# Up projection in groups of 512 columns over two sets of four PSUM banks

## The reference

```python
def conv_ffn(h, w_up, conv_w, conv_b, w_down):     # h (256, 2048), w_up (2048, 11264), w_down (5632, 2048)
    S = h.shape[1]
    u = h @ w_up
    up = jnp.pad(u, ((0, 0), (CONV_WIDTH - 1, 0), (0, 0)))          # CONV_WIDTH = 3
    u = sum(conv_w[j] * up[:, j:j + S] for j in range(CONV_WIDTH)) + conv_b
    a, b = jnp.split(u, 2, axis=-1)
    return (jax.nn.silu(a) * b) @ w_down
...
h = rms_norm(x, ffn_norm[l])
x = x + conv_ffn(h, w_ffn_up[l], ffn_conv_w[l], ffn_conv_b[l], w_ffn_down[l])
```

## Time and profile before

| | |
|---|---|
| median of 3 runs | 1080.18 us |
| profiled execution | 1080.29 us, span 1078.6 us |
| TensorE matmul busy | 1073.7 us (100%) |
| VectorE busy | 908.6 us (84%) |
| ScalarE busy | 633.9 us (59%) |
| DMA | 260.77 MB, mean 242 GB/s |
| up projection | 367 to 857 us of the span |
| down projection | 857 to 1075 us of the span |

### The profile page before, as it was taken

The page is one execution under the profiler, slowest core; times in us unless marked ns, Lnnn a source line. Parts: engine busy times, 40 slices in busy tenths (PEclk is TensorE's granted clock), DMA queues, the critical chain, the costliest instruction groups (busy, mean ns, idle before and its releaser), DMA issues.

```text
span 1078.6 us, 18188 instructions
## 1 busy us (share of the span) xinstructions
PE 1073.7 (100%) x6543; PEld 928.9 (86%) x6543; DVE 908.6 (84%) x1376; ACT 633.9 (59%) x930; POOL 79.8 (7%) x114
## 2 busy tenths in 40 slices
PE   9999999999999999999999999999999999999998
PEld 9888888888888889888888988888888888888887
DVE  7878988889655678888888888888877889999997
ACT  7677676757554655545555555545555566656663
POOL 4500000000000000000000000000000000000000
PEclk9999999999999999999999999999999999999999
DMA  8656687777889888798888888889888789798884
GB/s 275 183 163 176 190 229 223 216 223 222 234 258 245 278 236 235 240 256 239 249 232 243 237 255 245 227 258 247 271 240 235 218 282 319 256 309 315 260 289 163
DMA packets 192336, 260.77 MB, mean 242 GB/s; under 512 B 9605, under 2 KB 143894, under 8 KB 192022
## 3 DMA queue, kind: packets, MB, share of 16 engines
q1 hardware_dynamic: 176246, 216.24, 62.4%
q0 software_dynamic: 13344, 38.80, 17.6%
q10 hardware_dynamic: 2688, 5.00, 1.2%
HBM read 255.02 MB, written 43.78 MB: 277 GB/s over the span
## 4 chain that ended last, share of the span: by engine, by line
PE 99%; DMA 1%; DVE 0%; SPq 0%; issue 0%; DVEq 0%
PE bank L1821 38%; PE bank L1829 20%; PE bank L2216 7%; PE bank L2215 7%; PE bank L2214 7%; PE bank L2067 3%; PE bank L1868 3%; PE bank L2068 3%; PE bank L2069 3%; PE bank L1869 3%; PE bank L1870 3%; PE bank L1789 1%; PE bank L1897 1%; DMA xt<-in_x_dram 1%; PE bank L2106 0%; PE bank L1986 0%
## 5 line engine op out<-in xcount | busy, mean ns | idle before, releaser
L792 ACT CAST w_hi<-raw 128x1024 fp32r<-128x1024 f32 x299 | 311.9, 1048 | 252.7 <-PE bank L1829 118.4
L1201 DVE TENSOR_TENSOR w_lo<-raw,w_hi 128x1024 fp32r<-128x1024 f32 x299 | 363.8, 1222 | 108.1 <-ACT w_hi L792 107.5
L1821 PE MATMUL bank<-hs,w_hi 128*128 128x512 f32 x1792 | 423.0, 391 | 0.0
L1821 PEld LDWEIGHTS bank<-hs,w_hi 128*128 128x128 f32 x1792 | 331.3, 188 | 66.2 <-issue 0.9
L1829 PEld LDWEIGHTS bank<-hs,w_lo 128*128 128x128 f32 x1792 | 224.6, 192 | 5.7 <-issue 0.2
L1829 PE MATMUL bank<-hs,w_lo 128*128 128x256 f32 x1792 | 227.3, 283 | 0.0
L1171 ACT CAST hi_slot<-slot 128x1024 fp32r<-128x1024 f32 (+1 forms) x102 | 117.7, 1187 | 64.7 <-DVE slot L1746 25.2
L1728 DVE TENSOR_TENSOR slot_lo<-slot,hi_slot 128x1024 fp32r<-128x1024 f32 (+1 forms) x102 | 136.7, 1388 | 5.8 <-ACT hi_slot L1171 4.7
L2216 PE MATMUL bank<-hi_slot,gated 128*128 128x512 f32 (+1 forms) x194 | 75.1, 387 | 0.0
L2214 PE MATMUL bank<-hi_slot,gated 128*128 128x512 f32 (+1 forms) x194 | 75.1, 387 | 0.0
L1646 DVE SCALAR_TENSOR_TENSOR C<-U,cols,C 128x256 f32<-128x256 f32 x176 | 73.3, 478 | 0.0
(11 more groups left out here) (248 smaller groups left out, 1183.8 us busy)
## 6 DMA issues: line engine op xcount, KB each, us to landing
raw<-in_w_ffn_up_dram SPq DMA_DIRECT2D x176, 512.0 KB, 5.2
u_sums<-in_w_ffn_down_dram POOLq DMA_DIRECT2D x58, 512.0 KB, 6.7
raw<-in_w_in_dram SPq DMA_DIRECT2D x51, 512.0 KB, 4.5
slot<-in_w_ffn_down_dram SPq DMA_DIRECT2D x38, 512.0 KB, 5.0
slot<-u_sums SPq DMA_DIRECT2D x74, 256.0 KB, 5.6
raw<-in_w_in_dram SPq DMA_DIRECT2D x66, 256.0 KB, 4.2
raw<-in_w_out_dram SPq DMA_DIRECT2D x32, 512.0 KB, 5.7
u_sums<-u_sums POOLq DMA_DIRECT2D x16, 512.0 KB, 7.4
```

The lines of the kernel that those rows point to most:

```text
L792: act.copy(w_hi[:, i, :], raw[:, i, :]).then_inc(units_hi, 1)
L1201: dve.tensor_tensor(w_lo[:, i, :], raw[:, i, :], w_hi[:, i, :].bitcast(F32), ALU.subtract)\
L1821: m = pe.matmul(banks[b][:, :], w_hi[:, i, c], hs[:, 4 * i + k, :], start=(first and k == 0), stop=(final and k == 3))
```

## The change

The up projection is done in 11 pairs of groups. Four quads make a pair: two for a (512 channels), two for b. A wide quad is half of the 2048 rows by 512 columns (a unit is 2 row tiles by 512 columns, loaded in rows of 2 KB), so that the two quads of a add up in four banks (2, 3, 6, 7), and those of b in the other four (0, 1, 4, 5). The number of units, of matmuls and their sizes stay as they are. The last pair's b is done as before: two quads of 256 columns and all rows (groups 20 and 21), each into two banks. The works follow in the order a, a, b, b of a pair; the work with number w holds the splitting of quad w+3 (before: w+2), and the first three quads are split ahead of work 0. `C` has three tiles instead of two. Since a result is whole only after two quads, works w and w+1 of a both wait for the end of the second quad. The loops of ScalarE and VectorE are written out. TensorE's loop has 9 passes of four quads. In the down projection pair 0 adds up in banks 2, 3, 6, 7 and pair 1 in 0, 1, 4, 5; TensorE now waits ahead of q = 0 for the evacuations of a, and ahead of q = 0 to 3 for the `gated_lo` that they need. Ahead of the loop TensorE waits for the row of the second norm (`row_made`), which is now spread through bank 0.

```diff
-        C = sb_at(place, "C", [P, 2, 2, SEQ])
+        C = sb_at(place, "C", [P, 3, 2, SEQ])
+        banks_up = [[(bank[2], bank[3]), (bank[6], bank[7])], [(bank[0], bank[1]), (bank[4], bank[5])]]
+        banks_row = [bank[6], bank[0]]
-        sums_of = [[bank[4], bank[5], bank[6], bank[7]], [bank[0], bank[1], bank[2], bank[3]]]
+        sums_of = [[bank[2], bank[3], bank[6], bank[7]], [bank[0], bank[1], bank[4], bank[5]]]
...  # SyncE
-            with sp.Fori(0, UP_GROUPS) as g:
-                load_channels(g * 2 + Q_UP, w_up_v, g * GC)
-                load_channels(g * 2 + Q_UP + 1, w_up_v, g * GC + D_FF)
+            def load_wide(n, ab):
+                for half in range(2):
+                    for i in range(RING):
+                        load_unit(n * 4 + Q_UP + 2 * ab + half, i, w_up_v, 8 * half + 2 * i, 2, n * GT + ab * D_FF, GT)
+            with sp.Fori(0, UP_PAIRS - 1) as n:
+                for ab in range(2):
+                    load_wide(n, ab)
+            load_wide(UP_PAIRS - 1, 0)
+            for half in range(2):
+                load_channels(Q_DOWN - 2 + half, w_up_v, D_FF + (UP_GROUPS - 2 + half) * GC)
...  # ScalarE
+            for n in range(UP_PAIRS):
+                for g in (2 * n, 2 * n + 1):
+                    a_work(g, 2 * n + g)
+                    if g - 1 in range(RESIDENT_SUMS, SEVENS) and g % 2 == 0:
+                        park_sums(g - 1)
+                for g in (2 * n, 2 * n + 1):
+                    if g == UP_GROUPS - 1:
+                        act.wait_ge(sum_parked, 16 * PARKED_SUMS)
+                    b_work(g, 2 * n + g + 2)
...
+            def some_hi(quad, units):
+                for i in units:
+                    if quad < Q_DOWN + 2:
+                        make_hi(quad, i)
...  # VectorE
+            def taps(work, c_tile, ab, g, quad):
                 dst = U[:, :, 2:SEQ + 2]
+                last_narrow = ab == 1 and g == UP_GROUPS - 2
+                evacuate(banks_up[ab][g % 2], work, (Q_UP + 2 * (work // 2) + 2 - last_narrow) * RING, dst)
+                some_lo(quad, [0])
...
+            def b_work(g, work):
+                quad = work + Q_UP + 3
+                taps(work, 1, 1, g, quad)
                 dve.wait_ge(silu_a, g + 1)
+                dve.wait_ge(tap0, work * 2 + 2)
...
-            for g in range(SEVENS):
-                a_work(g, g * 2 + Q_UP + 2)
-                b_work(g, g * 2 + Q_UP + 3, sums_too=True)
-                lo_of_sums(g)
-            with dve.Fori(SEVENS, UP_GROUPS - 1) as g:
-                a_work(g, g * 2 + Q_UP + 2)
-                b_work(g, g * 2 + Q_UP + 3)
-            a_work(UP_GROUPS - 1, Q_DOWN)
-            b_work(UP_GROUPS - 1, Q_DOWN + 1)
+            for n in range(UP_PAIRS):
+                for g in (2 * n, 2 * n + 1):
+                    a_work(g, 2 * n + g)
+                for g in (2 * n, 2 * n + 1):
+                    b_work(g, 2 * n + g + 2)
+                    if g < SEVENS:
+                        lo_of_sums(g)
...  # TensorE
+            def high_wide(half, i, banks):
+                for k in range(2):
+                    for f in range(4):
+                        c = slice(k * GT + f * P, k * GT + (f + 1) * P)
+                        m = pe.matmul(banks[f // 2][f % 2][:, :], w_hi[:, i, c], hs[:, 8 * half + 2 * i + k, :],
+                                      start=(half == 0 and i == 0 and k == 0), stop=(half == 1 and i == 3 and k == 1))
+                return m
...
+            pe.wait_ge(row_made, 2)
+            for half in range(2):
+                quad_wide(Q_UP + 2 + half, half, banks_up[1])
+            with pe.Fori(1, UP_PAIRS - 1) as n:
+                for ab in range(2):
+                    pe.wait_ge(groups_evacuated, n * 4 + 2 * ab + G_UP)
+                    for half in range(2):
+                        quad_wide(n * 4 + 2 * ab + half + Q_UP, half, banks_up[ab])
+            pe.wait_ge(groups_evacuated, (UP_PAIRS - 1) * 4 + G_UP)
+            for half in range(2):
+                quad_wide(Q_DOWN - 4 + half, half, banks_up[0])
+            pe.wait_ge(groups_evacuated, (UP_PAIRS - 1) * 4 + 2 + G_UP)
+            for half in range(2):
+                quad_channels(Q_DOWN - 2 + half, banks_up[1][half])
...
+                    if pair == 0 and at == 0:
+                        pe.wait_ge(groups_evacuated, G_DOWN + BANK_PAIRS - 2)
+                    if pair == 0 and at < OLD_RING:
+                        pe.wait_ge(gated_lo, K_PAIR_AT[pair][at] + 1)
```

More of the change, by code:

```diff
@@ L859, in spread_row @@
                 act.wait_ge(row_spread, n + 1)
-                act.copy(x_rms_row[:, :], bank[6][:, 0:SEQ]).then_inc(row_made, 1)
+                act.copy(x_rms_row[:, :], banks_row[n][:, 0:SEQ]).then_inc(row_made, 1)
             spread_row(0)
@@ L1106, in a_work @@
[L1106 to L1112, removed]
-                act.activation(a, a, ACT.Silu).then_inc(silu_a, 1)
[L1114 to L1121, removed]
+                    act.activation(C[:, c_tile, c, :], U[:, c, 2:SEQ + 2], ACT.Identity,
+                                   scale=cols[:, col + conv_col(2):col + conv_col(2) + 1],
+                                   bias=cols[:, col + C_BIAS:col + C_BIAS + 1]).then_inc(tap2, 1)
@@ L1122, in b_work @@
+            def b_work(g, work):
+                quad = work + Q_UP + 3
+                some_hi(quad, [0])
+                last_tap(work, 1, 1, g)
+                some_hi(quad, [1, 2])
                 act.wait_ge(ab_made, g + 1 + FREE)
-                act.copy(gated[:, bass.ds(g * 2, 2), 0:SEQ], C[:, 1, :, :]).then_inc(gated_hi, 1)
-                make_hi(quad, 3)
+                act.copy(gated[:, g * 2:g * 2 + 2, 0:SEQ], C[:, 1, :, :]).then_inc(gated_hi, 1)
+                some_hi(quad, [3])
@@ L1202, in make_lo, with evacuate @@
                     .then_inc(units_split, 1)
-            def evacuate(group, n, units, dst):
+            def evacuate(banks, n, units, dst):
                 dve.wait_ge(units_used, units + RING)
-                b0, b1 = pair_of(group)
+                b0, b1 = banks
                 dve.tensor_reduce(dst[:, 0, :], b0[:, :].rearrange("p (h t) -> p t h", h=2), AX, ALU.add)
@@ L1634, in _, with some_lo @@
                 make_lo(Q_UP + 1, i)
+            for i in range(RING):
+                make_lo(Q_UP + 2, i)
             dve.wait_ge(row_made, 2)
-            def taps(n, ab, g, quad):
+            def some_lo(quad, units):
+                for i in units:
+                    if quad < Q_DOWN + 2:
+                        make_lo(quad, i)
+            def taps(work, c_tile, ab, g, quad):
                 dst = U[:, :, 2:SEQ + 2]
-                evacuate(G_UP + ab, n, (n + Q_UP + 1) * RING, dst)
-                make_lo(quad, 0)
+                last_narrow = ab == 1 and g == UP_GROUPS - 2
+                evacuate(banks_up[ab][g % 2], work, (Q_UP + 2 * (work // 2) + 2 - last_narrow) * RING, dst)
+                some_lo(quad, [0])
                 for tap, before, after in ((1, tap2, tap1), (0, tap1, tap0)):
@@ L1648, in taps, with a_work @@
                                                  ALU.mult, ALU.add).then_inc(after, 1)
[L1649 to L1657, removed]
+                some_lo(quad, [1])
+            def a_work(g, work):
+                taps(work, 2 * (g % 2), 0, g, work + Q_UP + 3)
+                some_lo(work + Q_UP + 3, [2, 3])
@@ L1844, in unit_channels, with low_wide, first_wide @@
                 last.then_inc(units_used, 1)
+            def high_wide(half, i, banks):
[5 more added lines that the diff above has]
+                return m
+            def low_wide(half, i, banks):
+                for k in range(2):
+                    for f in range(4):
+                        c = slice(k * GT + f * P, k * GT + (f + 1) * P)
+                        m = pe.matmul(banks[f // 2][f % 2][:, 0:SEQ], w_lo[:, i, c], hs[:, 8 * half + 2 * i + k, 0:SEQ],
+                                      start=False, stop=False)
+                return m
+            def first_wide(half, i, banks, in_the_middle=None):
+                pe.wait_ge(units_split, (Q_UP + half) * RING + i + 1 + RING)
+                if i % 2 == 0:
+                    high_wide(half, i, banks)
+                    last = low_wide(half, i, banks)
+                else:
+                    low_wide(half, i, banks)
+                    if in_the_middle is not None:
+                        in_the_middle()
+                    last = high_wide(half, i, banks)
+                last.then_inc(units_used, 1)
             def quad_channels(quad, banks):
@@ L1857, in quad_channels, with quad_wide @@
                     high(i, banks, False, i == RING - 1).then_inc(units_used, 1)
+            def quad_wide(quad, half, banks):
+                for i in (0, 1):
+                    pe.wait_ge(units_split, quad * RING + i + 1 + RING)
+                    high_wide(half, i, banks)
+                for i in (0, 1):
```

(27 more changed lines are left out.)

59 lines of the change are left out of this document (30 added, 29 removed).

## The result

The changed kernel takes 1084.12 us (median of 8 runs, 1083.62 to 1085.14) against 1080.18 for the one before (8 runs, 1080.04 to 1081.68): ratio 1.0035, 95% interval 1.0025 to 1.0046. It is 3.9 us slower; 1084.1 was forecast.

What follows compares the result with a forecast made beforehand. TensorE was taken as the bound, gapless in the up projection, with VectorE next. The other parts cost nothing; 3.8 us of down-projection lateness plus 0.1 for hops gave 1080.2 + 3.9 = 1084.1 us, range 1080.1 to 1086.5.

Steps and rivals of the forecast that it cites:

- TensorE's work in four banks: TensorE's matmuls taking turns in four banks: costed at nothing, bounds 1.1 us less or more.
- TensorE's waits, splitting ahead, front, loads: Up projection and its start: bank waits, earlier splitting and loads in 2 KB rows each cost nothing.
- Order a, a, b, b on VectorE: Up projection: two b works in succession use 2.4 us of a 3.9 us cover, so 0; 4 us without cover.
- The bare last work: VectorE at the up projection's end: last b work, with no splitting in it, takes 6.7 us.
- s = 877.5: Start of VectorE's split of q = 4's piece a in the down projection, 7.0 us later than 870.52.
- What reaches TensorE: Down projection: piece b of q = 11 late by 3.8 us, about 1.5 at q = 4; 0.1 more for hops.
- the slices: Down projection: TensorE's remaining lateness comes in slices of 0.5 us at q = 6, 7, 9, 10 and 11.
- the hidden case: Rival: the down projection's delay is hidden, time within 0.2% of before, 1080.2 if all hidden; chance 0.24, hidden or nearly.
- The second half of pair 0: Down projection: VectorE 4.9 us later there leaves 0.4 us of margin; pair 1 unchanged but for banks.
- Four banks faster: Rival: four banks save up to 36.6 us over 42 wide quads, 1047.5; chance 0.09, shared with unseen causes.
- Late data: Rival: loads behind SyncE's later wait come late, ScalarE waits at q = 6 to 8; 1085 to 1087; chance 0.08.
- The loop: Rival: TensorE's longer up-projection loop pass is fetched anew, 8 returns at 3.1 us cost 25 us, 1109; chance 0.04.

Runs made afterwards that it cites:

- loads moved: Changed kernel with SyncE's wait for the last gated_lo, the parked sums' load and x2's first part moved behind q = 7's loads: 1083.72 us, ratio 1.0032.
- wide end: Changed kernel with the last pair's b done wide like all others, instead of two groups of 256 columns: 1083.52 us, ratio 1.0032.
- end filled: Changed kernel with the last two b works worked into one another, nothing left out: 1080.01 us, ratio 1.0003.
- the kernel before, delayed: Kernel before the change plus idle VectorE products between its last b work and first down-projection split: 15 products 1084.02 us, 7 products 1080.35 us.
- the run with both edits: Changed kernel with group 14's sums parked inside group 15's b work and the last two b works worked into one another: 1079.89 us, ratio 0.9998.
- parked twice: Changed kernel with group 14's sums stored twice at the same place, ScalarE waiting between the two stores: 1091.88 us, ratio 1.0105.

## Why the prediction was right, point by point

- *TensorE's work in four banks: nothing.* Right. A quad is 11.11 us in the chain after as before.
- *TensorE's waits, splitting ahead, front, loads: nothing.* Right. The wait for the norm's row shows nowhere.
- *Order a, a, b, b on VectorE: nothing.* Right for VectorE. **Wrong by what moved with it on ScalarE.** I had read the order of the works and not the one DMA in it: of the two `park_sums`, the first went from between a and b work to just ahead of its own wait. It cost 0.5 us in the profile (843.09 against 842.56) and depended on the landing: 3.8 and 4.9 us left TensorE without a wait (loads moved, wide end), 5.6 and 5.7 made one of 0.5; 5.0 us (end filled) made none either. In the medians it is 0.3 to 0.5 us (1084.02 against 1083.5 to 1083.7), which the intervals don't resolve.
- *The bare last work, 6.7 us, s = 877.5.* Measured 871.05 to 877.73 = 6.7, and 878.00 less 0.53 = 877.5.
- *What reaches TensorE: 3.8 + 0.1, first 1.5 at q = 4.* Measured 3.96, with 1.4 to 1.6 at q = 4 and the slices where they were named. This term stands by itself: the kernel before, delayed, has 3.96 too, with nothing else changed.
- *The agreement of the whole, 1084.1 with 1084.12, is in part luck.* Two terms of half a microsecond each were missing, and they cancel: the 0.5 of the parked sums, and the 0.5 by which the last stores end sooner. In the medians the changed kernel without a parked wait is 3.3 to 3.6 above before, which is 3.96 less these stores, to 0.2 us. And the stated range, 1080.1 to 1086.5, took in the hidden case as well: by itself it would not have told the mechanism from none.
- *The second half of pair 0, with a margin of 0.4 us, and pair 1.* Held: no wait after q = 11.
- *Rivals.* Four banks faster: fell, by the run with both edits (1079.89, interval 0.9989 to 1.0007). Late data: fell, by the loads moved. Hidden: fell, by the result. The loop: fell; TensorE's nine passes run gapless, and the instruction queue q8 fetched 35 packets instead of 31. Eight returns of a pass of 512 would have added far more. By an estimate from the counts, the four packets (0.06 MB) are just the code that is now written out: 20 returns over 256 instructions became 8 over 512, so 1,024 more instructions are there once, 60 bytes each. The Trainium skill (Runtime: NRT & Kernel Launch, section on instruction fetch mechanics) has TensorE hold 2048 instructions, and a branch stall outside of two pages; for a pass of 512 the trace agrees with the first, and shows no stall as the second would have it.

## What to carry to other kernels

When the bound engine has no gap, a reordering can only cost; ask which engine is second, how many microseconds of lead it has where the stages meet, and add up what the new order leaves it to do there. A last piece of work with no other work in it costs its full latency, hops and waits included; fill it (here 3.9 us were won back by that alone). And when works are reordered, follow every DMA issue in them to its own wait. Afterwards account for the time place by place: a total that agrees can hold two errors that cancel, as here.

## What the runs showed of the hardware

- TensorE's clock fell within a wait of 6.1 us, and in no other profile here, in which TensorE's matmuls start 1.4 us late at most. Busy time by stretch, parked twice (columns as in the earlier trace rows):

```profile
757.00:760.00 3.00, 0.54 (x3) 0.11 (x1) 0.20 (x1) 0.95 (x3) 0.80 (x1) 1.00 0.59 96
760.00:763.60 3.60, 0.00 (x0) 0.00 (x0) 3.57 (x7) 1.73 (x4) 0.00 (x0) 0.71 0.57 113
763.60:765.00 1.40, 1.33 (x3) 1.14 (x4) 1.40 (x5) 1.00 (x2) 0.00 (x0) 0.50 0.21 20
765.00:766.40 1.40, 1.40 (x5) 1.02 (x4) 1.33 (x2) 1.17 (x2) 0.00 (x0) 0.50 0.78 240
766.40:768.00 1.60, 1.60 (x5) 1.31 (x4) 1.17 (x2) 1.35 (x2) 0.00 (x0) 0.50 0.92 319
768.00:770.00 2.00, 2.00 (x11) 1.65 (x11) 2.00 (x4) 0.00 (x0) 0.00 (x0) 0.91 1.02 291
```

  It was granted 0.50 (1.2 GHz) from before 763.6 to 768. The matmuls in between start 0.427 us apart instead of 0.227, without a gap, and the 16 took 5.95 us to the next line's start (769.62) where 3.75 is usual behind a wait. The clock cost 2.2 us; by the estimate above 0.8 of them would otherwise have been waited.
- Each wait of TensorE cost some 0.1 us on top: the matmul after the waiting one starts 0.34 us behind it instead of 0.23, in all six waits of the down projection.
- A store of 384 KB, issued at the same place, landed after 3.8 to 5.7 us in five profiles; issued twice in a row, after 5.3 and then 7.2 us.
